# The output projection of the convolution layer, over pairs of row tiles with seven block products for eight

## The chip, the cores and the metric

The kernel runs on one core of a Trainium2 chip. The metric is the device time of one execution in microseconds (us), as the median of three runs. One execution was also taken by the hardware profiler; every time in this text comes from that execution or from the three runs.

## What is computed

Two layers over 4096 tokens with 1024 channels: each has a mixer, a gated residual, a normalisation, and a mixture of experts. The mixer of the second layer is a short convolution, and its last projection is what the change touches:

```python
def short_conv_mixer(h, w_in, conv_w, w_out):
    b_g, c_g, v = jnp.split(h @ w_in, 3, axis=-1)
    u = c_g * v
    z = lax.conv_general_dilated(u, conv_w, ...)
    return (b_g * z) @ w_out
...
    x = x + (1 + g1)[:, None, :] * out
    hn = modulate(rmsnorm(x, norm2_g[i]), sh2, sc2)
    x = x + (1 + g2)[:, None, :] * hier_moe(hn, ...)
```

The router of the mixture takes `hn`, finds for each token a group and two experts, and writes records of them.

## The kernel before

The program is a chain of phases, each behind a barrier of all engines: constants, `ssm_front`, `ssm_scan`, `project` ("glu"), `moe` ("m0"), `conv_in` ("conv"), `project` ("cout"), `moe` ("m1"). The change touches `conv_in` and the second `project`. All products are in two parts: each operand is split into a high part (ScalarE copies it with rounding) and a low part (VectorE subtracts), and `product` (L140) gives three matmuls for one block of 128 x 128 by 128 x 512.

**conv_in.** It computes `h @ w_in`, the convolution and the gate `b_g`, and writes the result transposed to the DRAM tensor `zT`. Its second part is a list of `OPS` = 84 operations, n = 0 to 83, in 12 groups g of seven (r = n mod 7), 36 matmuls each: the first four groups are of column chunk 1, the next of chunk 2, the last of chunk 3. They are themselves seven products for eight (class `Seven`): the sums of the inputs are made by GpSimd (`combine`), sums of the weights too (`small_mix`). In each group VectorE adds banks into kept sums, and after r = 1, 4, 5 and 6 it has a column tile of z ready; GpSimd stores the four tiles (`store(g, 0)` to `store(g, 3)`). SyncE loads the operand of n + 4 when product n is through, ScalarE makes the high part of n + 2 during n, VectorE the low part. PSUM has two sets of three banks, so product n waits until VectorE has read what product n - 2 left. Near the end SyncE also loads the weight of the next phase (`n_raw`, eight slices, straight from the input `conv_w_out`), ScalarE and VectorE split it (L2689, L2988), and the first source tile likewise.

**project, "cout".** It runs over 32 tiles of 128 tokens. For each, TensorE makes two banks (`cout_pM`, 2 x 512 columns) of 8 products, that is 48 matmuls. VectorE multiplies by the gate `1 + g1` (L1447), adds the residual (L1449), squares and sums (L1451), normalises (L1459, L1461), and makes the low part of the next source tile (L1434). TensorE transposes the normalised rows (`turned_hn`, L1694) and multiplies them with the router (`router_halves` L1710, `router_sum` L1719). After every four tiles VectorE runs `choose` (a chain of some 35 small operations on the logits) and then, after two matmuls of TensorE (`batch_ranks`), `place`; GpSimd stores the records. The order on each engine is that of the code; each body is written out for all tiles.

## Time and profile before

| | us |
|---|---|
| median of three runs | 6161.75 |
| lowest, highest | 6160.59, 6164.22 |
| the profiled execution | 6154.4 |
| its span | 6152.6 |
| TensorE busy | 5849.7 (95% of the span) |
| VectorE busy | 3795.6 (62%) |
| GpSimd busy | 2086.2 (34%) |

Starts are in us from the span's start. The convolution's 84 operations run from 3494 to 4187, phase "cout" from 4196 to 4658, and the last mixture follows. A row of the timeline has start, duration, engine, line, operation, tiles, and in brackets how long the engine was idle before it and what ended that. TensorE's matmuls overlap: the distance from start to start is what one costs.

### The profile page before, as it was taken

What the parts mean: (1) busy time and instruction counts of PE and PEld (TensorE: products, weight loads), DVE (VectorE), ACT (ScalarE), POOL (GpSimd) and SP (SyncE); (2) the same over time, 40 slices, a digit from 0 to 9 for tenths busy, and PEclk for the clock granted to TensorE, in tenths of its full rate; (3) what the DMA queues carried; (4) which work ended last, traced back from release to release, by engine and by line L of the source; (5) the groups of instructions that cost most, each with busy time, mean ns of one, the idle gap of its engine ahead of it and who ended that gap; (6) DMA issues with size and microseconds to landing.
All of it is one profiled execution on the core that took longest, in us unless ns stands there. A gap on an engine that the chain in (4) does not pass through costs nothing. (4 is left out here: it accounts for less than half of the span.)

```text
span 6152.6 us, 83067 instructions
## 1 busy us (share of the span) xinstructions
PE 5849.7 (95%) x28274; PEld 4775.9 (78%) x28275; DVE 3795.6 (62%) x5360; ACT 2133.1 (35%) x3188; POOL 2086.2 (34%) x1978
## 2 busy tenths in 40 slices
PE   7999989999899999999989999998997999999994
PEld 5876668888678888888868788887775888888884
DVE  6889945554455555555536688876776554556555
ACT  2334432222144334444335323321113333444434
POOL 6555538870122222222324533101112222223222
PEclk9999999999899999999999999999998999999997
DMA  4564664432267666767647756644445656777767
GB/s 153 175 193 150 189 230 148 140 135 83 84 220 214 204 174 209 217 201 212 188 132 269 268 184 202 198 156 162 152 155 191 194 163 188 212 214 244 212 199 282
DMA packets 621295, 1152.42 MB, mean 187 GB/s; under 512 B 122708, under 2 KB 219572, under 8 KB 620089
## 3 DMA queue, kind: packets, MB, share of 16 engines
q1 hardware_dynamic: 422256, 799.04, 38.0%
q0 software_dynamic: 94176, 315.82, 18.8%
q10 hardware_dynamic: 104682, 35.19, 2.2%
q8 instruction: 109, 1.79, 0.1%
q14 instruction: 72, 0.59, 0.0%
HBM read 863.32 MB, written 286.29 MB: 187 GB/s over the span
## 5 line engine op out<-in xcount | busy, mean ns | idle before, releaser
L2288 DVE SCALAR_TENSOR_TENSOR m_o<-m_pO,m_weight_of,m_gate 128x512 f32<-128x512 f32 x316 | 233.6, 746 | 714.1 <-POOLq L1933 377.4
L2255 DVE TENSOR_TENSOR m_w_lo<-m_w_raw,m_w_hi 128x1024 fp32r<-128x1024 f32 x512 | 596.1, 1214 | 0.1
L1915 POOL COPY m_gather_now<-m_gather_of 128x1 int32 (+1 forms) x161 | 182.5, 1133 | 1147.0 <-DMA x<-m_o,m_scatter_now 913.7
L2086 ACT ACTIVATE m_xT_hi<-m_pX 128x512 fp32r<-128x512 f32 x320 | 191.4, 599 | 1000.3 <-PE m_pB L146 994.3
L144 PE MATMUL m_pA<-m_w_lo,m_xT_hi 128*128 128x512 f32 x1280 | 517.4, 404 | 14.2 <-DVE m_xT_lo L2266 14.2
L2074 ACT ACTIVATE m_w_hi<-m_w_raw 128x1024 fp32r<-128x1024 f32 x512 | 505.6, 1053 | 50.3 <-DMA m_w_raw<-in_moe_w_dram 29.2
L2027 PE MATMUL m_pO<-m_w_lo,m_hT_hi 128*128 128x512 f32 x1280 | 514.1, 402 | 0.4 <-ACT m_hT_hi L2091 0.2
L146 PE MATMUL m_pA<-m_w_hi,m_xT_hi 128*128 128x512 f32 x1280 | 503.0, 393 | 0.0
L145 PE MATMUL m_pA<-m_w_hi,m_xT_lo 128*128 128x512 f32 x1280 | 500.4, 391 | 0.0
L2027 PE MATMUL m_pO<-m_w_hi,m_hT_hi 128*128 128x512 f32 x1280 | 499.9, 391 | 0.0
L144 PE MATMUL m_pB<-m_w_lo,m_xT_hi 128*128 128x512 f32 x1280 | 498.3, 389 | 0.0
L146 PE MATMUL m_pB<-m_w_hi,m_xT_hi 128*128 128x512 f32 x1280 | 498.2, 389 | 0.0
L145 PE MATMUL m_pB<-m_w_hi,m_xT_lo 128*128 128x512 f32 x1280 | 498.1, 389 | 0.0
L144 PE MATMUL glu_pM<-glu_w_lo,glu_sT_hi 128*128 128x512 f32 x1024 | 409.6, 400 | 2.8 <-DVE glu_w_lo L1542 2.8
L145 PE MATMUL glu_pM<-glu_w_hi,glu_sT_lo 128*128 128x512 f32 x1024 | 401.1, 392 | 0.0
L146 PE MATMUL glu_pM<-glu_w_hi,glu_sT_hi 128*128 128x512 f32 x1024 | 400.2, 391 | 0.0
L144 PE MATMUL conv_p<-conv_op_lo,conv_w_hi 128*128 128x512 f32 x1008 | 392.7, 390 | 5.6 <-DVE conv_op_lo L2922 5.6
L145 PE MATMUL conv_p<-conv_op_hi,conv_w_lo 128*128 128x512 f32 x1008 | 392.3, 389 | 0.0
L146 PE MATMUL conv_p<-conv_op_hi,conv_w_hi 128*128 128x512 f32 x1008 | 392.3, 389 | 0.0
L2261 DVE TENSOR_TENSOR m_w_lo<-m_w_raw,m_w_hi 128x1024 fp32r<-128x1024 f32 x256 | 306.2, 1218 | 74.8 <-issue 63.4
L1401 POOL DMA_INDIRECT slots<-route_record,route_place x120 | 124.6, 1038 | 662.7 <-DVEq L1527 628.4
L2031 PE MATMUL m_pO<-m_w_hi,m_hT_lo 128*128 128x512 f32 x1280 | 342.6, 390 | 0.0
(531 smaller groups left out, 13591.2 us busy)
## 6 DMA issues: line engine op xcount, KB each, us to landing
m_w_raw<-in_moe_w_dram SPq DMA_DIRECT2D x384, 1024.0 KB, 7.4
conv_op_raw<-xr SPq DMA_DIRECT2D x84, 1024.0 KB, 5.4
glu_ada<-in_ada_w_dram POOLq DMA_DIRECT2D x96, 256.0 KB, 3.2
a_x<-in_x_dram SPq DMA_DIRECT2D x32, 512.0 KB, 3.4
a_ada<-in_ada_w_dram POOLq DMA_DIRECT2D x64, 256.0 KB, 3.4
s_u<-u SPq DMA_DIRECT2D x64, 256.0 KB, 2.7
s_r<-k SPq DMA_DIRECT2D x64, 256.0 KB
glu_x<-in_x_dram SPq DMA_DIRECT2D x32, 512.0 KB, 5.0
```

The costliest lines, as they stand in the source:

```text
L144: pe.matmul(out, lh, rl, start=start, stop=False)
L145: pe.matmul(out, ll, rh, start=False, stop=False)
L146: return pe.matmul(out, lh, rh, start=False, stop=stop)
L1401: pool.indirect_dma_start(slots_dram, bass.IndirectOffsetOnAxis(ap=routes.place[b % 2][:, j:j + 1], axis=0), routes.record[b % 2][:, j, :] ...
L1915: pool.tensor_copy(gx[:], gidx[:, bass.ds(t, 1)]).then_inc(gi_ready, 1)
L2027: pe.matmul(pO[:, n, :], hT_hi[:, k, :], w[:, n, k, :], start=k == 0 and w is w2_low, stop=False)
L2031: last = pe.matmul(pO[:, n, :], hT_lo[:, k, :], w2_high[:, n, k, :], start=False, stop=k == KF - 1)
L2074: act.activation(W13[s][2][:, m, k:k + 2, :], W13[s][0][:, m, k:k + 2, :], ACT.Copy).then_inc(w13_hi, 1)
L2086: act.activation(xT_hi[:, 4 * q:4 * q + 4, :], pX[:, 4 * q:4 * q + 4, :], ACT.Copy).then_inc(xt_hi, 1)
L2255: tt(W13[s][1][:, m, k:k + 2, :], W13[s][0][:, m, k:k + 2, :], W13[s][2][:, m, k:k + 2, :].bitcast(F32), ALU.subtract).then_inc(w13_lo, 1)
L2261: tt(w2_low[:, n, k:k + 2, :], w2_raw[:, n, k:k + 2, :], w2_high[:, n, k:k + 2, :].bitcast(F32), ALU.subtract).then_inc(w2_lo, 1)
L2288: dve.scalar_tensor_tensor(out=ob[:, n, :], in0=pO[:, n, :], scalar=wslot[:, bass.ds(tile_, 1)], in1=gate2[:, n, :], op0=ALU.mult, op1=ALU ...
```

## The change

For each pair of tiles (2p, 2p + 1) the projection is a 2 x 2 by 2 x 2 product of blocks: rows are the odd and the even tile, the inner dimension its two halves of 512, columns the two halves of the output. The changed kernel makes it with seven block products (84 matmuls) for eight (96).

- **Weights.** The block operands (four blocks of the weight and four sums, each [512, 512]) are made by GpSimd during the convolution, in 16 steps `turn(i)`, four in each of the groups 7 to 10, with the factor `1 + g1` multiplied in, and written to the new DRAM tensor `wt`. A step waits until both stores of the step before it have landed, loads two pieces of the weight and a piece of the gate, computes six operations, and stores twice.
- **The end of conv_in.** SyncE waits at n = 78 for the last of these stores, and then loads the weights 0 and 1 of the seven, then the operand of n = 83, and later weights 2 and 3 and two source tiles. ScalarE splits weight 0 at n = 79, 1 at 81, 2 at 82, VectorE behind it; weights 3 to 6 are split in the next phase, 4 to 6 also loaded there.
- **The projection** is a new function `project_out`. Four banks of 512 columns go round; product m waits until bank m - 4 is read. VectorE makes four sums of source tiles, seven low parts, and the sums over banks straight into the residual rows; it no longer multiplies by the gate. The sum of squares goes to ScalarE. The routing is as before, in other places: both tiles of pair p - 1 are turned and routed during pair p, `choose` in slot 3 and `place` in slot 6 of the odd pairs from p = 3 on. After the last pair both of its tiles are still to be normalised and routed.

Core of the diff (of `project_out`, which is new, the parts of VectorE and TensorE):

```diff
@@ conv_in, GpSimd
+            def turn(i):
+                kk, q = seven.turns[i]
+                (a, b_), tt = pieces, pool.tensor_tensor
+                for h in range(2):
+                    if i:
+                        pool.wait_ge(turn_st[h], 16 * i)
...
+                for h in range(2):
+                    pool.dma_start(a[:, 2 * h:2 * h + 2, :], next_view[kk][q][h]).then_inc(turn_ld, 16)
+                pool.dma_start(gate_piece[:], gate_view[q].broadcast_to([P, 2, P])).then_inc(turn_ld, 16)
+                pool.wait_ge(turn_ld, 48 * i + 48)
+                d = Chain(pool, turn_step, 6 * i)
+                d(pool.tensor_scalar(gate_piece[:], gate_piece[:], 1.0, None, ALU.add))
+                wide = a[:].rearrange("p (h n) f -> p h n f", h=2)
+                d(tt(wide, wide, gate_piece[:].unsqueeze(1).broadcast_to([P, 2, 2, P]), ALU.mult))
+                to = lambda o: wt_dram[o:o + 4, kk, :, q * P:(q + 1) * P].rearrange("o p f -> p o f")
+                pool.dma_start(to(0), a[:]).then_inc(turn_st[0], 16)
+                d(tt(b_[:, 3, :], a[:, 3, :], a[:, 1, :], ALU.subtract))
+                d(tt(b_[:, 1, :], a[:, 1, :], a[:, 0, :], ALU.subtract))
+                d(tt(b_[:, 0, :], b_[:, 3, :], a[:, 0, :], ALU.add))
+                d(tt(b_[:, 2, :], a[:, 2, :], b_[:, 0, :], ALU.subtract))
+                pool.dma_start(to(4), b_[:]).then_inc(turn_st[1], 16)
...
+                for i in range(4 * (g - 7), 4 * (g - 6)) if 7 <= g < 11 else ():
+                    turn(i)
+                    if i % 4 == 1:
+                        store(g, 2)
@@ conv_in, SyncE
                 if n == OPS - 6:
-                    for k in range(6):
-                        sp.dma_start(n_raw[:, k, :], next_view[k]).then_inc(n_w_ld[k], 16)
+                    for q in range(2):
+                        sp.wait_ge(turn_st[q], 16 * len(seven.turns))
+                    next_weights(0)
+                    next_weights(1)
@@ conv_in, ScalarE   (NEXT_W = {OPS - 5: 0, OPS - 3: 1, OPS - 2: 2})
-                ks = {OPS - 3: range(0, 6), OPS - 2: range(6, KD)}.get(n, ())
...
+                if n in NEXT_W:
                     act.wait_ge(prod, 3 * n)
+                    act.wait_ge(n_w_ld[NEXT_W[n]], 16)
+                    act.activation(ahead.w_hi[NEXT_W[n]][:], ahead.w_raw[NEXT_W[n]][:], ACT.Copy).then_inc(n_w_hi, 1)
@@ project_out, VectorE
+            def slot(p, s):
+                q, r = next_left(p, s)
...
+                if s == 0:
+                    if p:
+                        left_sums(p, 4)
+                        odd_done(p - 1)
+                        low(p, 6)
+                        normed(p - 1, 0)
...
+                elif s == 3:
+                    from_bank(p, 2, u2[:], kept[:])
+                    if more:
+                        low(q, r)
+                    if batch_at(p) is not None:
+                        choose(batch_at(p))
...
+                else:
+                    from_bank(p, 5, xe[:, B], xe[:, B])
...
+                    if p:
+                        out_logits(2 * (p - 1))
+                    if batch_at(p) is not None:
+                        place(batch_at(p))
@@ project_out, TensorE
+            def turned_hn(n):
+                pe.wait_ge(hn_ready, n + 1)
+                if n:
+                    pe.wait_ge(lg_out, n)
+                if n % 2 and batch_at((n + 1) // 2) is not None:
+                    pe.wait_ge(r_out, batch_at((n + 1) // 2) + 1)
...
+                    if p and r == 6:
+                        turned_hn(2 * (p - 1) + 1)
```

Three places where instructions move. On GpSimd in `conv_in`, from the stores of group 6 on (`conv_z` is a column tile, `ws` takes weight sums of the convolution). Before:

```order
L2855 DMA ws<-conv_small_15309 256x1x256
L2834 DMA zT<-conv_z 128x512 x20
L2478 UNCONDITIONAL_BRANCH
```

and now, from the same store on through the first step and a half (`conv_piece` holds the four pieces, `wt` is the new tensor):

```order
L3409 DMA ws<-conv_small_15352 256x1x256
L3364 DMA zT<-conv_z 128x512 x4
L3383 DMA conv_piece_15391<-in_conv_w_out_dram 128x2x128 x2
L3384 DMA conv_gate_piece<-mod 128x2x128
L3387 TENSOR_SCALAR conv_gate_piece<-conv_gate_piece 128x256
L3389 TENSOR_TENSOR conv_piece_15391<-conv_piece_15391,conv_gate_piece 128x512
L3391 DMA wt<-conv_piece_15391 128x4x128
L3392 TENSOR_TENSOR conv_piece_15392<-conv_piece_15391 128x128
L3393 TENSOR_TENSOR conv_piece_15392<-conv_piece_15391 128x128
L3394 TENSOR_TENSOR conv_piece_15392<-conv_piece_15392,conv_piece_15391 128x128
L3395 TENSOR_TENSOR conv_piece_15392<-conv_piece_15391,conv_piece_15392 128x128
L3396 DMA wt<-conv_piece_15392 128x4x128
```

GpSimd had nothing but twenty stores left; now 16 such steps stand between them.

On SyncE at the end of `conv_in`. Before, and then now (`conv_op_raw` is the operand of one of the 84 operations, n = 81 to 83 here):

```order
L2551 DMA conv_op_raw1_15337<-xr 128x4x512
L2551 DMA conv_op_raw2_15338<-xr 128x4x512
L2591 DMA ahead_raw_49<-in_conv_w_out_dram 128x1024 x6
L2551 DMA conv_op_raw3_15339<-xr 128x4x512
L2594 DMA ahead_raw_49<-in_conv_w_out_dram 128x1024 x2
```

```order
L3072 DMA conv_op_raw1_15380<-xr 128x4x512
L3072 DMA conv_op_raw2_15381<-xr 128x4x512
L3075 DMA ahead_w_raw0_49<-wt 128x4x512
L3075 DMA ahead_w_raw1_52<-wt 128x4x512
L3072 DMA conv_op_raw3_15382<-xr 128x4x512
L3121 DMA ahead_src0_91<-zT 128x8x128
```

The weight loads ahead of the last operand now read what GpSimd writes.

On ScalarE there, before and then now (`conv_op_hi` is a high part; slots 2 and 3 are n = 82 and 83):

```order
L2633 ACTIVATE conv_op_hi1_15345<-conv_op_raw1_15337 128x1024 x2
L2633 ACTIVATE conv_op_hi2_15346<-conv_op_raw2_15338 128x1024 x2
L2633 ACTIVATE conv_op_hi3_15347<-conv_op_raw3_15339 128x1024 x2
L2689 ACTIVATE ahead_hi_51<-ahead_raw_49 128x1024 x6
```

```order
L3164 ACTIVATE conv_op_hi1_15388<-conv_op_raw1_15380 128x1024 x2
L3218 ACTIVATE ahead_w_hi0_51<-ahead_w_raw0_49 128x2048
L3164 ACTIVATE conv_op_hi2_15389<-conv_op_raw2_15381 128x1024 x2
L3222 ACTIVATE ahead_left_hi0_72<-ahead_src0_91 128x512
L3222 ACTIVATE ahead_left_hi1_75<-ahead_src0_91 128x512
L3164 ACTIVATE conv_op_hi3_15390<-conv_op_raw3_15382 128x1024 x2
```

The first weight's high part has come ahead of the operands of n = 82 and 83; on VectorE its low part stands ahead of their low parts in the same way.

## Rows read from the trace of the kernel before

**Rows 1.** Busy time by engine, phase "cout" without its first tile; clock last but two.

```profile
4214.00:4640.00 426.00, 416.91 (x2320) 337.02 (x2320) 302.97 (x600) 74.36 (x152) 60.77 (x56) 1.00 0.45 151
```

**Rows 2.** Timeline of VectorE in phase "cout".

```profile
4348.14 1.22 DVE L1447 TENSOR_TENSOR cout_acc<-cout_pM,cout_gate 128x1024 f32<-128x1024 f32 x1 [1.89 <-PE cout_pM L146]
...
4383.22 0.17 DVE L1489 TENSOR_REDUCE cout_m<-cout_logits 128x4 f32<-128x16 f32 x1
...
4390.71 1.22 DVE L1447 TENSOR_TENSOR cout_acc<-cout_pM,cout_gate 128x1024 f32<-128x1024 f32 x1
...
4402.83 1.22 DVE L1447 TENSOR_TENSOR cout_acc<-cout_pM,cout_gate 128x1024 f32<-128x1024 f32 x1 [1.87 <-PE cout_pM L146]
...
4407.50 1.29 DVE L1459 SCALAR_TENSOR_TENSOR cout_hn<-cout_x,cout_stat,cout_gain 128x1024 f32<-128x1024 f32 x1
...
4416.12 1.22 DVE L1447 TENSOR_TENSOR cout_acc<-cout_pM,cout_gate 128x1024 f32<-128x1024 f32 x1 [4.84 <-PE cout_pM L146]
```

**Rows 3.** Timeline of TensorE in phase "cout", one tile and the end of another.

```profile
4399.68 0.39 PE L146 MATMUL cout_pM<-ahead_hi,next_src_hi 128*128 128x512 f32 x1
...
4402.40 0.39 PE L146 MATMUL cout_pM<-ahead_hi,next_src_hi 128*128 128x512 f32 x1
4402.63 1.03 PE L1694 MATMUL cout_pH<-ident,cout_hn 128*128 128x128 f32 x8
...
4415.93 1.03 PE L1694 MATMUL cout_pH<-ident,cout_hn 128*128 128x128 f32 x8
```

**Rows 4.** Timeline of VectorE at the end of `conv_in` and the start of "cout".

```profile
4186.57 0.68 DVE L2971 TENSOR_TENSOR conv_c<-conv_p,conv_kept 128x512 f32<-128x512 f32 x1
4187.17 0.68 DVE L2971 TENSOR_TENSOR conv_v<-conv_p,conv_kept 128x512 f32<-128x512 f32 x1
4187.88 0.69 DVE L2979 TENSOR_TENSOR conv_u<-conv_c,conv_v 128x512 f32<-128x512 f32 x1
...
4191.63 0.69 DVE L2984 TENSOR_TENSOR conv_z<-conv_z,conv_b 128x512 f32<-128x512 f32 x1
4195.76 3.59 DVE L1530 TENSOR_TENSOR ahead_lo<-ahead_raw,ahead_hi 128x1024 fp32r<-128x1024 f32 x3 [3.44 <-PEq L105]
```

**Rows 5.** Timeline of GpSimd: `store(7, 1)` and `store(10, 1)`.

```profile
3944.57 0.54 POOL L2834 DMA_DIRECT2D zT<-conv_z  x1 [23.94 <-DVE conv_z L2984]
...
4115.92 0.54 POOL L2834 DMA_DIRECT2D zT<-conv_z  x1 [23.94 <-DVE conv_z L2984]
```

**Rows 6.** Groups of GpSimd in `conv_in`: count, busy us, mean ns, idle before.

```profile
L2809 POOL TENSOR_TENSOR conv_mix<-conv_mix 128x512 f32<-128x512 f32 x16 | 24.6, 1536 | 1.3
...
L2852 POOL TENSOR_TENSOR conv_small<-conv_small 128x128 f32<-128x128 f32 x24 | 20.2, 840 | 1.9
...
L2855 POOL DMA_DIRECT2D ws<-conv_small x24 | 16.7, 695 | 7.9 <-POOL conv_small L2854 7.9
L2851 POOL TENSOR_TENSOR conv_small<-conv_small 128x128 f32<-128x128 f32 x24 | 15.5, 646 | 6.7 <-DMA conv_small<-in_conv_w_in_dram 6.5
```

**Rows 7.** DMA issues: count, KB each, median us from issue to landing.

```profile
conv_op_raw<-xr SPq DMA_DIRECT2D x84, 1024.0 KB, 5.4
...
conv_small<-in_conv_w_in_dram POOLq DMA_DIRECT2D x48, 128.0 KB, 3.2
ws<-conv_small POOLq DMA_DIRECT2D x24, 256.0 KB, 2.8
```

**Rows 8.** TensorE after a pause: timeline in `conv_in` and the last mixture, and a window.

```profile
3533.49 0.50 PE L144 MATMUL conv_p<-conv_op_lo,conv_w_hi 128*128 128x512 f32 x1 [3.37 <-DVE conv_op_lo L2922]
...
6072.10 1.11 PE L2015 MATMUL m_pH<-ident,m_h 128*128 128x128 f32 x4 [4.22 <-DVE m_h L2274]
...
6072.00:6076.00 4.00, 3.76 (x10) 2.82 (x11) 2.16 (x6) 3.10 (x7) 0.53 (x1) 0.50 1.01 406
```

**Rows 9.** The end of "cout": TensorE after its last products, and VectorE's last operation.

```profile
4634.79 1.03 PE L1694 MATMUL cout_pH<-ident,cout_hn 128*128 128x128 f32 x8
...
4658.19 0.17 DVE L1526 CAST route_place<-route_place_f 128x8 int32<-128x8 f32 x1
```

More of the change, by code:

```diff
@@ L1275, in project @@
     records_of = lambda b: 16 * sum(len(routes.columns(c)) for c in range(b % 2, b + 1, 2))
[L1276 removed]
+    pad_st = sem("pad_stored")
     with ExitStack() as ctx:
@@ L1535, in _ @@
             chosen(dve.tensor_scalar(routes.base[:], io32[:], float(T), None, ALU.mult))
-            if glu:
-                low(0, 0)
-            else:
-                dve.sem_inc(tlo[0], 1)
-            for q in range(KD if glu else 0):
+            low(0, 0)
+            for q in range(KD):
                 dve.wait_ge(w_hi_ready, q + 1)
@@ L1654, in products @@
                 pe.wait_ge(tlo[s], i + 2)
-                if not glu:
-                    pe.wait_ge(out_read, n + 1)
-                elif not (isinstance(n, int) and n == 0):
+                if n != 0:
                     pe.wait_ge(gated, 2 * n)
-                first, second = ((1, 0), (2, 0)) if glu else ((0, KD // 2), (1, 0))
                 def rest():
@@ L2433, in __init__ @@
         assert not sums and not mixes
+        self.turns = [(kk, q) for kk in range(KH) for q in range(4)]
         self.small = [(c, kk, j) for c in range(2, CHUNKS) for kk in range(KH) for j in range(3)]
@@ L2582, in _ @@
                 again = seven.sb(n) == SUPER - 1 and seven.chunk(n) + 1 < NC_
-                if more or again or n in (OPS - 6, OPS - 4):
+                if more or again or n in range(OPS - 6, OPS - 2):
                     sp.wait_ge(prod, 3 * n + 3)
@@ L2867, in _ @@
                         store(g, 1)
+                for i in range(4 * (g - 7), 4 * (g - 6)) if 7 <= g < 11 else ():
+                    turn(i)
+                    if i % 4 == 1:
+                        store(g, 2)
+                if g not in range(7, 11) and g + 1 < OPS // SEVEN:
+                    store(g, 2)
                 if g + 1 < OPS // SEVEN:
-                    store(g, 2)
                     store(g, 3)
@@ L2998, in _ @@
                     all_mixed(dve, 1)
-                ahead = n + 2 < OPS
-                if ahead:
+                follows = n + 2 < OPS
+                if follows:
                     op_low(n + 2, 0)
@@ L3004, in _ @@
                         summed(n, i, r - 2, kept[r - 1][JS[i]])
-                        if ahead and i == 0:
+                        if follows and i == 0:
                             op_low(n + 2, 1)
@@ L3018, in _ @@
                     column_out(n, q, base + first + 3 * by)
-                elif ahead:
+                elif follows:
                     op_low(n + 2, 1)
```

719 lines of the change are left out of this document (580 added, 139 removed).

## The prediction, made before the changed kernel ran

> **What bounds the kernel now.** I read the busy times by stretch first. In phase "cout" TensorE is busy 416.91 of 426 us at full clock and VectorE 302.97 [rows 1]: TensorE bounds, VectorE has 29% left. TensorE's timeline gives the prices. Between 4399.68 and 4402.40 lie 12 matmul starts, so a matmul costs 0.227 us; a tile takes 13.30 us [rows 3], of which 48 matmuls are 10.9 and the routing (8 transposes, 16 + 2 small products, changes between them) 2.4. VectorE's timeline shows the rest: an ordinary tile keeps it 13.29 - 4.84 = 8.45 us; `choose` runs from 4383.22 to 4390.71, 7.5 us, and the tile with `place` takes 12.12 - 1.87 = 10.25, so `place` is 1.8 [rows 2]. From 4348.14 to 4402.83, four tiles with one `choose`, pass 54.7 us and not 4 x 13.3 = 53.2: the chain behind `choose` already costs TensorE 1.5 us. In the convolution's last groups TensorE bounds too, an operation being 36 x 0.227 = 8.16 us, a group of seven 57.1, which GpSimd's stores confirm: (4115.92 - 3944.57) / 3 = 57.1 [rows 5]. GpSimd is idle between them. So there are two questions: does TensorE remain the bound of the projection, and do the new steps on the idle GpSimd end in time.
>
> **The steps on GpSimd.** `turn(i)` hides nothing of its own latency: loads, operations, stores and the next step's first wait follow one another. Its parts: three DMA issues, the last 1.1 us after the first (0.54 each, as [rows 5]), and 3.2 until it lands [rows 7], 4.3; one operation on 256 columns and one on 512, between 0.65 and 0.84 for 128 columns and 1.54 for 512 [rows 6], so 0.8 + 1.4, 0.3 before the store's issue; the issue 0.7 [rows 6]; four operations of 128 columns at a mean of 0.65 to 0.84, with gaps 3.2; 0.3, and 2.8 until the second store lands [rows 7]. Sum 13.8; the stores here are in pieces half as long, I add 0.4: **14.2 us**. With every part at its shortest I get 11.6, with queues 15.5.
>
> Four steps and the four stores of z among them, 56.8 + 2.2 = 59.0, against a group of 57.1: the steps of group 7 begin at 3945.1 (behind `store(7, 1)`), those of 8, 9 and 10 each 1.9 late or later. The last store lands at R = 3945.1 + 3 x 59.0 + 57.4 = 4179.5. SyncE, however, waits for it from n = 78, whose product is through at about 4145.6 (that of n = 74 ended some 3 us before `store(10, 1)` at 4115.92, and four operations of 8.16 follow). Behind that wait stand weight 0, weight 1, and the operand of n = 83; behind weight 0 stands ScalarE at n = 79, ahead of the operand of n = 82; behind ScalarE VectorE. So operation 82, due three operations later at 4170, cannot start before R and what follows. From R on: weight 0 lands after 5.4 [rows 7], with two loads behind it 6.4; its high part takes ScalarE 2.0 (no row has 2048 columns; VectorE's 1024 take 1.2 [rows 4]); then VectorE is the chain. It has three low parts of weights at 2.3, 6.9; four halves of operands at 1.14, 4.6; three column tiles at 4186.57 to 4192.32, 5.75 each [rows 4], 17.3; six more bank sums and two source low parts at 0.6, 4.8; 33.6 in all. Then 3.4 to the next phase [rows 4]. It starts at R + 45.4 = 4224.9 instead of 4195.7: **+29.2 us**. The bounds follow from the step: at 11.6 nothing slips from group to group, R = 4116.5 + 47.0 = 4163.5, and the phase starts 13.2 late; at 15.5, R = 4200 and it starts 50 late. Were the steps done by 4145, the start would be 2.3 early, since VectorE has one weight to split at n = 82 for three slices before. I take 14.2, nearest to the median landings.
>
> Here the Trainium skill speaks for a shorter step ("DMA: Bandwidth & Descriptors", section "Anatomy of one DMA"): it gives a DMA about 2.0 us fixed and bytes at 436 GB/s. By that, 128 KB would be 2.3 and 256 KB 2.6, the step 12.7 and the phase 17.6 late, not 29.2; the trace's landings of 3.2 and 2.8 are longer, and the sum goes by them.
>
> **The projection.** Removed from TensorE: 12 matmuls in a pair, 2.72 us, over 16 pairs 43.6. That is hidden unless VectorE keeps up. Its queue for a pair, by start-to-start distances of 512 columns: 0.60 where the next one doesn't wait for it (4186.57 to 4187.17), 0.71 to 0.73 where it does [rows 4], some 0.1 more where a semaphore is raised between. Seven low parts 4.2; four sums of sources 2.6, and behind the third 0.7 in which ScalarE makes the high part that the next low part needs; seven reads of banks 4.9; kept and second sums 2.7; two normalisations of 1.29 + 1.22 and a small one, 5.3 [rows 2]; logits 0.2. In all **20.7 us a pair**, against TensorE's 84 x 0.227 + 4.8 = 23.9. But two pairs hold a `choose` and a `place`: VectorE 50.7, TensorE 47.8. And the waits couple the two closely: TensorE may not turn the second tile of pair p - 1 (behind product 6 of pair p) before VectorE's `out_logits` and, in odd pairs, the start of `place` in its slot 6. So an odd pair is VectorE's: 20.7 + 7.5 + 0.4 = 28.6 from such a turn to the next, in which TensorE stands about 4.3 us in one piece; an even pair is TensorE's, 24.0. Two pairs: **52.6** against 54.7 before.
>
> The phase: from its start to the turn in pair 2 about 79 us (the first seven products wait for weights 4, 5 and 6, whose low parts are ready near 15, 19 and 24 us, by 1 MB loads at 5.4 and more and 2.3 on VectorE for each; pair 1 is then VectorE's). Then seven odd and six even pairs, 200.2 + 144.0, to 423. The tail: before, 4634.79 to 4658.4, 23.6 [rows 9]. Now both tiles of the last pair are still to be normalised and routed: one normalisation more (2.7) and the short `choose` of two tiles (6.4) stand on the chain that was hidden, less 1: 31.7. The phase is 455 us, before 4658.4 - 4195.7 = 462.7: **-7.7**. The bound below is a TensorE at 47.8 for two pairs throughout; that is a rival. Above: 10 us more at the start if loads take the longer times.
>
> **TensorE's clock.** A pause of 3.37 us left it at full clock; behind one of 4.22 the granted clock was 0.50 in 6072 to 6076 [rows 8], that is 1.2 of 2.4 GHz, and nine matmuls at twice the distance, with slower transposes, cost 2.2 us. The new pauses of about 4.3 us, eight with that of pair 1, lie at that edge, and the even pair after each is TensorE's, so such a loss counts. I take half of them: **+9**, between 0 and 18.
>
> **The sum**, on the profiled execution's own time of 6154.4: + 29.2 - 7.7 + 9 = 6184.9; its median over runs lies 7.35 higher, so **6192 us**.
>
> **Rivals.**
> - *Steps in time.* If four steps end within some 30 us behind `store(10, 1)`, SyncE waits for nothing, the phase starts 2.3 early, and the projection with the clock is about even: 6161. For it: GpSimd is empty, and the shortest small operations and landings. Against: the sum of even the shortest parts is 11.6, four of them 47.
> - *The projection is TensorE's after all*, the one on the other side: VectorE's two pairs fall below 47.8 us. Then 8 x 4.9 = 39 less and no pauses: 6192 - 39 - 9 = 6144, faster in spite of the late steps. It decides at 3 us in 50.7, 6% of VectorE's work; for it speaks that VectorE's chained operations may overlap more than I let them; against, that rows of the same width repeat within 0.01 us.
> - *All pauses lower the clock, and the steps take 15 us or more*: 50 - 7.7 + 18, and the start's 10: 6222 at the worst, 6207 as its middle. The Trainium skill ("TensorE: Matmul & The Clock Gate", section "Why this matters for your kernels") warns of this: bursts of matmuls with pauses between fall to half clock each time. The row at 4.22 agrees, the one at 3.37 doesn't.
> - *The waits of VectorE on the stores of z.* `store(g, 3)` now stands behind four steps. With 59 us a group it lands some us before VectorE needs the tile again; with 62 it doesn't, and the delay adds to the third rival.
>
> **How the numbers follow.** Late steps and VectorE-bound pairs 0.62; the third rival 0.14; steps in time 0.15; TensorE-bound 0.07; the remaining 0.02 for less than 6149. The likeliest gives 6192. Its own range, from R at 11.6 us a step without losses of clock (6154.4 + 7.35 + 13.2 - 7.7 - 5 = 6162) to 15.5 with half of them (6215), is also where 8 in 10 lie: **6160 to 6215**. A measurement of this kernel tells about 0.2%, 12 us, from no change. Faster than 6149.4: 0.07 + 0.02, of which some ends above, 0.07. Within: most of "steps in time" and the low end of the likeliest, 0.17. Slower than 6174: 0.76.
>
> **What would show it.** Right: the four `turn` steps of a group last 50 to 60 us; SyncE's load of weight 0 starts after 4163 and TensorE is idle before operation 82; phase "cout" starts after 4208; in the odd pairs from 3 on TensorE has one pause of 4 to 5 us before the transposes, and VectorE none; two pairs take 52 to 53 us. Wrong: a step of 10 us or less (the first part falls); VectorE idle in the odd pairs, or 48 us for two (the second falls); a clock of 1.00 behind all pauses takes 9 us off, 0.50 behind each puts 9 on.

## The result

The changed kernel takes 6222.7 us in the median of four runs (6216.3 to 6232.8), the kernel before 6161.3 beside it: 1.0100 times as long (95% interval 1.0083 to 1.0118), **61.4 us slower**. Slower was forecast, but as 6192 (6160 to 6215): half the size. The profiled execution of the changed kernel took 6223.35 us, with a span of 6221.4 against 6152.6. The 68.8 us between the two profiles fall so:

| | forecast | measured |
|---|---|---|
| already there at `store(7, 1)`, ahead of the first step | 0 | 3.5 |
| later start of phase "cout", less that | +29.2 | +62.1 |
| the phase, from the barrier ahead of it to the first product of the last mixture, with the clock | -7.7 + 9 | +1.2 |
| the last mixture | 0 | +2.0 |

The 3.5 lie ahead of the first step. That they belong to the change isn't shown: among the experiments below, kernels whose code up to this point is the same have it anywhere from 3948.8 to 3955.1, and the profiled execution of the kernel before, at 6154.4, is 6.2 us below the lowest of its three runs.

First the steps. Timeline of GpSimd (start, duration, engine, line, what, and in brackets the idle time before and what ended it): the first step with the start of the second, then the last step.

```profile
3948.10 0.54 POOL L3364 DMA_DIRECT2D zT<-conv_z  x1 [23.94 <-DVE conv_z L3543]
3948.65 1.44 POOL L3383 DMA_DIRECT2D conv_piece<-in_conv_w_out_dram  x2
...
3955.38 0.94 POOL L3387 TENSOR_SCALAR conv_gate_piece<-conv_gate_piece 128x256 f32<-128x256 f32 x1 [4.59 <-DMA conv_gate_piece<-mod]
...
3962.95 0.78 POOL L3396 DMA_DIRECT2D wt<-conv_piece  x1 [0.29 <-POOL conv_piece L3395]
3969.83 1.42 POOL L3383 DMA_DIRECT2D conv_piece<-in_conv_w_out_dram  x2 [6.10 <-DMA wt<-conv_piece]
...
4203.61 1.42 POOL L3383 DMA_DIRECT2D conv_piece<-in_conv_w_out_dram  x2 [2.74 <-DMA wt<-conv_piece]
...
4208.46 0.85 POOL L3387 TENSOR_SCALAR conv_gate_piece<-conv_gate_piece 128x256 f32<-128x256 f32 x1 [2.73 <-DMA conv_gate_piece<-mod]
...
4214.14 0.80 POOL L3396 DMA_DIRECT2D wt<-conv_piece  x1 [0.29 <-POOL conv_piece L3395]
```

The first step takes 21.2 us, the last, until its stores have landed, 13.6. The four steps of groups 7 to 10 begin at 3948.65, 4020.11, 4092.11 and 4158.41: 71.5, 72.0 and 66.3 us for a group that I had at 59.0 and that the convolution passes in 57.1 [rows 5]. What happens behind the last store, SyncE, ScalarE, VectorE and TensorE:

```profile
4217.24 0.91 SPq L3075 DMA_DIRECT2D ahead_w_raw<-wt  x2
...
4222.91 1.91 ACT L3218 ACTIVATE ahead_w_hi<-ahead_w_raw 128x2048 fp32r<-128x2048 f32 x1 [64.75 <-DMA ahead_w_raw<-wt]
...
4224.86 2.29 DVE L3547 TENSOR_TENSOR ahead_w_lo<-ahead_w_raw,ahead_w_hi 128x2048 fp32r<-128x2048 f32 x1 [47.35 <-ACT ahead_w_hi L3218]
...
4230.07 0.80 PE L143 MATMUL conv_p<-conv_op_lo,conv_w_hi 128*128 128x512 f32 x1 [38.65 <-DVE conv_op_lo L3481]
...
4261.36 0.76 PE L143 MATMUL cout_p<-ahead_w_lo,ahead_left_hi 128*128 128x512 f32 x1 [12.19 <-PEq L104]
```

The chain is the one forecast: the last store lands and SyncE passes its wait at R = 4217.2, weight 0 lands, ScalarE, VectorE, and only then operation 82, for which TensorE stood 38.65 us. The phase starts at R + 44.1; the forecast was R + 45.4. R itself was forecast as 4179.5. Ahead of that VectorE had waited twice for a store of z behind the steps, 15.0 and 15.6 us, and TensorE behind it, 5.5 and 7.0; since the last step ends later still, this costs nothing more:

```profile
4158.32 0.49 DVE L3456 TENSOR_SCALAR conv_z<-conv_u,conv_taps 128x512 f32<-128x512 f32 x1 [15.59 <-DMA zT<-conv_z]
```

```profile
4161.16 0.79 PE L143 MATMUL conv_p<-conv_op_lo,conv_w_hi 128*128 128x512 f32 x1 [6.98 <-DVE conv_b L3530]
```

Now the projection. TensorE's turns of the second tile of pairs 2 and 14, and the busy times of the same middle of the phase as [rows 1] (PE, PEld, DVE, ACT, POOL; clock last but two):

```profile
4345.01 1.04 PE L2187 MATMUL cout_pH<-ident,cout_hn 128*128 128x128 f32 x8
...
4668.93 1.03 PE L2187 MATMUL cout_pH<-ident,cout_hn 128*128 128x128 f32 x8
```

```profile
4345.00:4450.00 105.00, 99.02 (x536) 79.54 (x535) 91.76 (x186) 37.69 (x68) 19.66 (x16) 0.93 0.45 152
4450.00:4560.00 110.00, 103.75 (x571) 83.48 (x570) 96.42 (x195) 41.41 (x76) 19.41 (x16) 0.97 0.48 162
```

Six times two pairs in 323.9 us, **54.0 us for two pairs** (four at 54.3 to 54.5, two at 53.2) against 52.6 forecast and 54.7 before [rows 2]. VectorE is busy 87% of the time, 71% before [rows 1]. An odd pair, TensorE:

```profile
4365.70 0.39 PE L145 MATMUL cout_p<-ahead_w_hi,ahead_left_hi 128*128 128x512 f32 x1
4369.08 0.64 PE L2210 MATMUL cout_pH<-cout_selector,cout_logitsT 100*128 100x36 f32 x2 [2.99 <-ACT cout_logitsT L2110]
...
4370.38 0.77 PE L143 MATMUL cout_p<-ahead_w_lo,ahead_left_hi 128*128 128x512 f32 x1
4370.95 0.63 PE L144 MATMUL cout_p<-ahead_w_hi,ahead_left_lo 128*128 128x512 f32 x1
...
4375.22 0.45 PE L145 MATMUL cout_p<-ahead_w_hi,ahead_left_hi 128*128 128x512 f32 x1
```

There is one pause, but not where I had it (before the transposes behind product 6): it is at `router_sum` behind product 5, and 2.99 us long. Behind it matmuls lie 0.43 apart and not 0.23, eleven of them: half of the full clock, 1.2 and not 2.4 GHz (the granted clock is 0.55 as a mean from 4369 to 4376). ScalarE's queue tells why, with VectorE's beside it:

```profile
4368.23 0.63 ACT L2080 ACTIVATE ahead_left_hi<-ahead_left_raw 128x512 fp32r<-128x512 f32 x1 [7.80 <-DVE ahead_left_raw L1933]
4368.77 0.26 ACT L2110 ACTIVATE cout_logitsT<-cout_pH 100x128 f32<-100x128 f32 x1
```

```profile
4358.01 0.16 DVE L1879 TENSOR_REDUCE cout_m<-cout_logits 128x4 f32<-128x16 f32 x1
...
4365.31 0.17 DVE L1904 TENSOR_SCALAR route_record<-route_token 128x8 f32<-128x8 f32 x1
...
4367.51 0.69 DVE L1933 TENSOR_TENSOR ahead_left_raw<-ahead_src,ahead_src 128x512 f32<-128x512 f32 x1
```

`choose` holds VectorE from 4358.01 to 4365.5, so the sum for block 3 of the next pair (L1933) is late; ScalarE waits 7.80 us for it with the high part (L2080), and the copy that TensorE wants (L2110) stands behind.

### The profile page after: what moved, and what is told of

It is laid out like the page before. It is cut to its first block and busy times, and to the rows that moved or that the text cites. A ratio compares the mean times of both kernels' runs of the same rounds, so it can differ in the third digit from the quotient of the medians.

```text
span 6221.4 us, 83117 instructions
## 1 busy us (share of the span) xinstructions
PE 5840.9 (94%) x28082; PEld 4760.3 (77%) x28083; DVE 3883.0 (62%) x5503; ACT 2219.2 (36%) x3316; POOL 2230.7 (36%) x2153
## 5 line engine op out<-in xcount | busy, mean ns | idle before, releaser
L2574 ACT ACTIVATE m_w_hi<-m_w_raw 128x1024 fp32r<-128x1024 f32 x512 | 505.7, 1053 | 49.7 <-DMA m_w_raw<-in_moe_w_dram 27.9
L2766 DVE TENSOR_TENSOR m_xT_lo<-m_pX,m_xT_hi 128x512 fp32r<-128x512 f32 x320 | 220.2, 689 | 184.0 <-ACT m_xT_hi L2586 184.0
```

Of the source, the lines that this page charges most:

```text
L2574: act.activation(W13[s][2][:, m, k:k + 2, :], W13[s][0][:, m, k:k + 2, :], ACT.Copy).then_inc(w13_hi, 1)
L2766: tt(xT_lo[:, 4 * q:4 * q + 4, :], pX[:, 4 * q:4 * q + 4, :], xT_hi[:, 4 * q:4 * q + 4, :].bitcast(F32), ALU.subtract).then_inc(xt_lo, 1)
```

## The experiments

Theory: the loss is the length of the steps and nothing else, and the projection is bound by VectorE. All kernels below come from the changed one; e2 to e7 and e9 to e11 also have the spread steps of e1, and each diff shows only what is new against the kernel named. Beside them the kernel before had 6160.9 (e0 to e3), 6162.2 (e4 to e7) and 6159.9 us (e8 to e11). "The phase" is from the barrier ahead of it to the first product of the last mixture: 464.1 us before, 465.3 changed. (In the changed kernels the phase's first product follows the barrier at once; in the kernel before it came 4.4 us later, at 4200.08.)

### Steps: e0, e1, e8

**e0_loads_ahead** has the loads of step i + 1 ahead of the work of step i:

```diff
+                if i + 1 < len(seven.turns):
+                    turn_load(i + 1)
-                pool.wait_ge(turn_ld, 48 * i + 48)
+                pool.wait_ge(turn_ld[i % 2], 48 * (i // 2) + 48)
```

> The changed kernel with one edit on GpSimd: the pieces have two pairs of buffers, and a step issues the loads of the step after it before it computes; the 16 steps stay in groups 7 to 10. My theory is that the length of a step sets the delay of phase cout. A step is now its issues (2.1), six operations (some 5.5 with gaps) and two stores' issues (1.6) without the waits for its load and for the stores of the step before: about 10 us for 16.8. Then no group slips, the last store lands near 4165, SyncE passes its wait 52 us earlier than 4217, phase cout starts at 4209 for 4261, and the run takes 6170 us (6160 to 6182) for 6223. Rival: the delay lies in the transfers (1 MB operands and pieces share the DMA engines) and in what stands behind SyncE's wait; then a shorter step gains less than half of it, and the run stays above 6195.

Measured 6190.9 us (6188.2 to 6199.2): between the two. My step was wrong: the loads of step i + 1 use the buffers of step i - 1, whose stores have only just been issued. The wait for the load is gone, the one for the stores is longer, as GpSimd's timeline shows (last store of a step, start of the next), and a step beside the convolution still takes 15.9 us. SyncE's first load of a weight and TensorE's first product of the phase below it:

```profile
3966.85 0.78 POOL L3411 DMA_DIRECT2D wt<-conv_piece  x1 [0.30 <-POOL conv_piece L3410]
3974.77 1.42 POOL L3390 DMA_DIRECT2D conv_piece<-in_conv_w_out_dram  x2 [7.14 <-DMA wt<-conv_piece]
...
4194.80 0.91 SPq L3077 DMA_DIRECT2D ahead_w_raw<-wt  x2
...
4239.00 0.77 PE L143 MATMUL cout_p<-ahead_w_lo,ahead_left_hi 128*128 128x512 f32 x1 [12.72 <-PEq L104]
```

What the theory says of everything behind the steps holds: R is 22.4 us earlier, the phase starts 22.4 earlier, at R + 44.2.

**e1_turns_early** spreads the steps:

```diff
-                for i in range(4 * (g - 7), 4 * (g - 6)) if 7 <= g < 11 else ():
-                    turn(i)
...
+                        if g in (3, 7, 8, 9):
+                            turn(turned_)
+                            turned_ += 1
                         store(g, 0)
+                        if g in (1, 2, 3, 5, 6, 7, 8, 9):
+                            turn(turned_)
+                            turned_ += 1
                         store(g, 1)
+                if g in (3, 7, 8, 9):
+                    turn(turned_)
+                    turned_ += 1
```

> The changed kernel with the 16 steps unchanged but spread: two buffers of their own, and one step in each of groups 1, 2, 5 and 6, three in each of groups 3, 7, 8 and 9, so that the last ends near 4110. Theory: SyncE waits for nothing at n = 78, phase cout starts at 4197 to 4200, all of the late steps' cost is gone and the projection is what remains: +62 of the +61 us lie in the steps, the projection with its clock losses is within 3 us of the old one, and the run takes 6158 us (6150 to 6166), as the kernel before. Rival: the steps also cost VectorE or the DMA queues something in the convolution wherever they stand: then 6170 or more. In the trace the projection keeps two pairs of 54.4 us with one pause of 2.99 us each.

Measured 6159.0 us (6156.3 to 6164.8), 0.9995 times the kernel before (0.9986 to 1.0005). The phase starts at 4201.3 and takes 465.0, the changed kernel's 465.3. (Expected was a start at 4197 to 4200; counted from `store(7, 1)`, 248.3 us against 251.2 in the kernel before, it is 2.9 early.) So the whole 61 us of the change are the steps that end late, and with them in time the projection gains nothing. The rival, a cost of the steps wherever they stand, is not seen.

**e8_three_a_group** is a dose between: `{3: 4, 7: 3, 8: 3, 9: 3, 10: 3}` steps by group, all behind `store(g, 1)`.

> The changed kernel with the 16 steps unchanged, in their own buffers, four in group 3 and three in each of the groups 7 to 10, all behind store(g, 1) as before. It is a dose between e1_turns_early (none late) and the changed kernel (four a group). Theory: three steps of 17 us and the stores take 53 us, less than a group of 57.1, so that no group slips; the last three begin near 4120 and end near 4171, SyncE passes its wait there, and phase cout starts 44.2 us later, as it did behind 4217.2 and 4194.8: 4213 to 4218, 15 us after that of e1_turns_early; run 6171 to 6178 us. Rival: the first late step costs as much as all four (the pause and its clock are the price, not its length): 6200 or more; or nothing, 6160.

Measured 6177.2 us (6173.0 to 6181.3), in the range. R is 4173.4, the phase starts at 4217.4, R + 44.0. Over all three doses each us of R is one us of the kernel: from the changed kernel to e8 R is 43.9 us earlier and the median 45.4 lower. The one between is not on this line: R falls by 22.4 to e0 and by 21.4 from there, the median by 31.8 and 13.7. R is read in one execution, and e0's, at 6199.2, is the slowest of its four; between the profiled executions the differences are 24.2 and 24.0.

### The order of the projection: e2, e3, e4, e7, e9

**e2_scalar_order** (from e1):

```diff
-                if s == 5 and p:
+                if p and s == (4 if batch_at(p) is not None else 5):
                     out_lT(2 * (p - 1))
```

> As e1_turns_early, and in the odd pairs with choose ScalarE copies the routing sums (cout_logitsT) ahead of the high part of the next pair's block 3, which waits for VectorE behind choose. It is this order at which TensorE pauses 2.99 us now. Theory: VectorE is the bound of the odd pair whatever ScalarE does; the pause goes to the transposes behind product 6, which wait for place, about 3.4 us long, with the same loss of clock behind it; two pairs stay at 53.5 to 54.5 us and the run within 4 us of e1_turns_early. Rival: the pause was ScalarE's order alone; then two pairs take 48 to 50 us, and the run 30 to 40 us less than e1_turns_early.

Measured 6165.6 us (6158.4 to 6168.1), 6.6 more than e1 where at most 4 were expected; two pairs take 54.0 to 54.9. The pause did go to the transposes, 4.07 us long. **e3_own_banks** (from e2) takes away this wait:

```diff
+        pL, pR = (core.ps(ctx, f"{tag}_{n}", [P, 4, P]) for n in ("pL", "pR"))
...
             def turned_hn(n):
                 pe.wait_ge(hn_ready, n + 1)
-                if n:
-                    pe.wait_ge(lg_out, n)
-                if n % 2 and batch_at((n + 1) // 2) is not None:
-                    pe.wait_ge(r_out, batch_at((n + 1) // 2) + 1)
```

> As e2_scalar_order, and the routing's sums, logits and ranks have two PSUM banks of their own, so that TensorE's transposes wait neither for VectorE's reading of the logits nor for place. Theory: what is left is the amount of VectorE's work, 50.8 us in two pairs (54.4 less the 3.6 that it is idle in the even pair) against TensorE's 47.8; two pairs take 51 to 52 us, pauses get short, most of the clock's loss of 2.6 us in a pair is gone, and the run takes 15 to 20 us less than e2_scalar_order. Rival: another wait takes the place of it (a bank, a low part) with the same pause: 54 us, no gain. A result of 48 us in two pairs would say that VectorE's work was never the bound.

Measured 6164.6 us (6160.1 to 6167.7), two pairs 54.7: no gain, the rival. **e4_scalar_order2** (from e3) takes away the wait that came in its place:

```diff
+                late = batch_at(p - 1) is not None
+                if s == 0 and p >= 2 and late:
+                    out_h(2 * (p - 2) + 1)
                 if s == 0 and p:
                     high(p, 6)
-                    if p >= 2:
+                    if p >= 2 and not late:
                         out_h(2 * (p - 2) + 1)
```

> As e3_own_banks, and behind an odd pair with choose ScalarE copies the turned rows (cout_hT) ahead of the high part of block 6, which waits for VectorE. In e3_own_banks TensorE paused 4.93 us for this copy. Theory: with this no queue stands between TensorE and its own work, only the amount of VectorE's work, 50.8 us in two pairs, is left, and two pairs take 51 to 52 us instead of 54.75; run 6142 to 6150 us. Rival: the pause moves again at the same size (54.5 or more, 6164 us): then each reordering only chooses where TensorE waits for the same VectorE, and the odd pair's surplus and the clock behind the pause set the time, not the sum over two pairs.

Measured **6142.5 us** (6139.5 to 6148.4), 0.9972 (0.9960 to 0.9983). The pause of an odd pair in e2, e3 and e4 (the last two pairs later), TensorE:

```profile
4311.91 1.30 PE L2187 MATMUL cout_pH<-ident,cout_hn 128*128 128x128 f32 x5 [4.07 <-DVEq L1912]
```

```profile
4312.93 1.87 PE L2203 MATMUL cout_pL<-cout_hT,cout_router 128*36 128x128 f32 x16 [4.93 <-ACT cout_hT L2108]
```

```profile
4360.54 1.07 PE L2206 MATMUL cout_pL<-cout_hT,cout_router 128*36 128x128 f32 x16 [1.21 <-ACT cout_hT L2108]
```

The pause went from `router_sum` to the transposes (waiting for `place`), and from there to the routing's product (waiting for ScalarE behind VectorE's sum), each time a little longer; with the third wait gone it is 1.2 to 1.6 and 1.3 us in two pieces, the clock stays full, and two pairs take 51.2 us. That is close to VectorE's own work as estimated, 50.8. The first two edits gave nothing without the third; whether the third would give it without them is not tested.

**e9_split_alone** cuts `choose` in two (below) on top of e4, with all work still on VectorE.

> As e4_scalar_order2 with choose cut in two as in e6_choose_split, but the sums of source tiles stay on VectorE. Theory (the sum of VectorE's work over two pairs is the bound): 50.8 to 51.3 us for two pairs as in e4_scalar_order2, run 6139 to 6146 us, since nothing leaves VectorE. Rival (the odd pair's surplus was the bound, and the cut is what helped in e6_choose_split): two pairs at 49.5 us or less and the run at 6130 us or less.

Measured 6141.7 us (6138.2 to 6147.5), two pairs 51.2. As the theory has it: moving work between pairs gives nothing while its sum is the bound.

**e7_filler** (from e1) asks what the clock alone costs:

```diff
+                        if batch_at(p) is not None and p + 1 < PAIRS:
+                            for k in range(11):
+                                pe.matmul(fill[:], w_hi[0][:, k % KH, 0:P], w_hi[0][:, k % KH, :], start=True, stop=True)
                         router_sum(2 * (p - 1))
```

> As e1_turns_early (not the ones behind it), and TensorE makes 11 more matmuls of 512 columns, 2.5 us, into a bank that nobody reads, just where it pauses 2.99 us in the odd pairs. It does the same work otherwise. Theory on the clock: the pause of 2.99 us costs twice, itself and then 2.4 to 2.6 us because the next 12 matmuls take 0.427 instead of 0.227 us; with the filler the pause is 0.5 us, the clock stays at 1.00, and two pairs take 51.6 to 52 us instead of 54.4; the run takes 13 to 17 us less than e1_turns_early, 6142 to 6146 us. Rival (VectorE is the bound of both pairs together, so a faster TensorE only waits elsewhere): less than 5 us. Second rival: the clock falls all the same, since VectorE and not TensorE's idleness brings it down: no gain at all.

Measured 6156.4 us (6154.6 to 6160.4), the phase 460.2 for 465.0. TensorE in one odd pair:

```profile
4308.95 0.41 PE L2210 MATMUL cout_pH<-cout_selector,cout_logitsT 100*128 100x36 f32 x2 [0.49 <-ACT cout_logitsT L2110]
...
4313.45 1.06 PE L2187 MATMUL cout_pH<-ident,cout_hn 128*128 128x128 f32 x8 [0.80 <-DVEq L1912]
...
4317.94 1.07 PE L2202 MATMUL cout_pH<-cout_hT,cout_router 128*36 128x128 f32 x16 [0.64 <-ACT cout_hT L2106]
```

The clock was full throughout (1.00 from 4283 to 4608), but of the 2.4 us of slow matmuls only 1.2 come back: with fast matmuls TensorE meets two new waits on VectorE's side, 0.80 and 0.64. Two pairs take 53.2, not 51.6 to 52. The run is 2.6 us under e1 and not 13 to 17: the first rival, less than 5. The clock cost 4.8 us of the phase in these two profiled executions, and 2.6 between the medians (3.9 if each is set against the kernel before beside it).

### Work off VectorE: e5, e6, e10, e11

**e5_sums_gpsimd** (from e4) moves the four sums (L1925 to L1938) to GpSimd.

```diff
                     if more:
                         low(q, r)
-                        left_sums(q, 1)
-                        left_sums(q, 2)
...
+            for p in range(1, PAIRS):
+                left_sum(p, 4)
+                for which in (1, 2) if p + 1 < PAIRS else ():
+                    left_sum(p + 1, which)
```

> As e4_scalar_order2, and GpSimd makes the four sums of source tiles of each pair from the second on, with its 512-column operations of some 1.5 us (6 of 24 us a pair). VectorE loses 5.3 us of 50.8 in two pairs and the waits of 0.7 for the high parts behind its own sums. Theory (VectorE's work is the bound): TensorE's 47.8 us is the bound of two pairs, with a short pause in the odd pair: 48 to 50 us, the run 6120 to 6135 us, clearly under the kernel before. Rival: VectorE and GpSimd slow each other (in the convolution an operation of VectorE took 1.69 for 1.22 us beside GpSimd's), or a sum comes late: two pairs stay above 51.5 us and the run above 6145.

Measured 6145.9 us (6142.0 to 6147.8): no gain, two pairs 52.4. The rival, and in both of its halves. A sum comes late: GpSimd makes the third one behind its eight stores of records, and in every two pairs VectorE waits once for ScalarE's high part of it:

```profile
4433.86 0.69 DVE L1976 TENSOR_TENSOR ahead_left_lo<-ahead_left_raw,ahead_left_hi 128x512 fp32r<-128x512 f32 x1 [2.93 <-ACT ahead_left_hi L2111]
```

And the two engines slow each other. Groups of VectorE from 4392 to 4500 (count, busy us, mean ns, idle before), e4 and then e5:

```profile
L1943 DVE TENSOR_TENSOR ahead_left_lo<-ahead_left_raw,ahead_left_hi 128x512 fp32r<-128x512 f32 x8 | 5.5, 693 | 3.4 <-ACT ahead_left_hi L2082 2.8
L1952 DVE TENSOR_TENSOR cout_x_even<-cout_p,cout_x_even 128x512 f32<-128x512 f32 x8 | 5.5, 682 | 0.0
L1959 DVE SCALAR_TENSOR_TENSOR cout_hn<-cout_x_odd,cout_stat,cout_gain 128x1024 f32<-128x1024 f32 x4 | 5.1, 1286 | 0.1
L1959 DVE SCALAR_TENSOR_TENSOR cout_hn<-cout_x_even,cout_stat,cout_gain 128x1024 f32<-128x1024 f32 x4 | 5.1, 1285 | 0.1
```

```profile
L1976 DVE TENSOR_TENSOR ahead_left_lo<-ahead_left_raw,ahead_left_hi 128x512 fp32r<-128x512 f32 x8 | 8.5, 1058 | 6.5 <-ACT ahead_left_hi L2111 5.9
L1992 DVE SCALAR_TENSOR_TENSOR cout_hn<-cout_x_even,cout_stat,cout_gain 128x1024 f32<-128x1024 f32 x4 | 8.4, 2111 | 0.1
...
L1985 DVE TENSOR_TENSOR cout_x_even<-cout_p,cout_x_even 128x512 f32<-128x512 f32 x8 | 5.5, 682 | 0.0
```

Operations of VectorE that read two tiles in SBUF grow where GpSimd works beside them: 0.69 to 1.06, 1.29 to 2.11 (the same normalisation of the odd row, in another place, keeps its 1.29). Those that read a bank (L1952, L1985) do not. Over the four groups that grow it is 10.4 us in 108, where the sums taken away were 12.4. Counted over whole pairs nothing is left of the gain: VectorE is busy 46.7 us in two pairs in e4 and 46.7 in e5. The Trainium skill states such a lock ("SBUF — State Buffer", section "SBUF: two separate sides": an operation of VectorE with two SBUF inputs and one of GpSimd hold a pair of ports in turn, for a whole instruction); the rows agree.

**e11_idle_adds** (from e4) measures that price alone, with four additions a pair on a buffer of no use.

```diff
+                pool.wait_ge(prod, 7 * p)
+                for _ in range(3):
+                    e(pool.tensor_tensor(idle[:], idle[:], idle[:], ALU.add))
...
+                pool.wait_ge(prod, 7 * p + 4)
+                e(pool.tensor_tensor(idle[:], idle[:], idle[:], ALU.add))
```

> As e4_scalar_order2, and GpSimd makes four additions of 512 columns in each pair on a buffer that nobody uses. It measures alone what such an operation costs VectorE, on which nothing waits here. Theory: while GpSimd's operation runs, a VectorE operation with both inputs in SBUF is held until it ends; eight of them in two pairs lengthen VectorE's work by about 0.6 us each, 5 us, as the rows of e5_sums_gpsimd had it (low parts 1.06 for 0.69, normalisation 2.11 for 1.29): two pairs 55 to 57 us for 51.2, run 6165 to 6180 us. Rival: the longer operations in e5_sums_gpsimd were those that waited for a sum: then 51.2 and 6142 us here.

Measured 6162.2 us (6159.0 to 6168.3), 19.7 more than e4, and 54.15 us for two pairs, 2.95 more: under the expected 55 to 57, but not the rival's 51.2. The lock is there though nothing waits for these operations; each of the eight costs 0.37 us, less than the 0.6 that I took from e5. VectorE's busy time in two pairs goes from 46.7 to 49.7 and the two pairs longer by the same, which shows that VectorE sets their time. (The stores of records stand between the additions here; they are the same ones as in e4.)

```profile
L1955 DVE TENSOR_TENSOR ahead_left_lo<-ahead_sum,ahead_left_hi 128x512 fp32r<-128x512 f32 x9 | 8.6, 957 | 0.3
L1955 DVE TENSOR_TENSOR ahead_left_lo<-ahead_left_raw,ahead_left_hi 128x512 fp32r<-128x512 f32 x8 | 6.1, 768 | 3.4 <-ACT ahead_left_hi L2094 2.8
```

**e6_choose_split** (from e5):

```diff
                     if batch_at(p) is not None:
-                        choose(batch_at(p))
+                        choose(batch_at(p), (0,) if p < PAIRS - 1 else (0, 1))
+                    if place_at(p) is not None and p < PAIRS - 1:
+                        choose(place_at(p), (1,))
```

> As e5_sums_gpsimd, and choose is cut in two: the part that reads the logits (3.1 us) stays in slot 3 of the odd pair, the rest (4.3 us) and place come in the even pair behind it. VectorE then has some 21.2 us in the odd and 24.3 us in the even pair against TensorE's 23.9 in each. Theory: no pause of TensorE above 1 us in the middle of the phase, granted clock 1.00 there, two pairs 47.8 to 48.5 us, run 6112 to 6125 us. Rival: the odd pair's surplus was absorbed by the four banks already in e5_sums_gpsimd: no difference between the two.

Measured **6130.3 us** (6124.4 to 6134.8), 0.9949 (0.9932 to 0.9966), above the 6112 to 6125 expected. Two pairs take 48.2 and 48.5 at first and 49.4 from pair 7 on: no pause of TensorE is over 0.5 us between 4250 and 4590, and VectorE is busy 93% of the time. Against e9, which differs only in who makes the sums, that is 1.8 us less in two pairs and 11.4 in the run, although VectorE is as busy as there (46.7 for 46.8 in two pairs); what is shorter is its idle time, 2.8 for 4.5, of which 1.4 were the two waits for ScalarE's high part behind its own sums. What is left between 49.4 and TensorE's 47.8 I did not take apart. **e10_records_last** puts the stores of records behind the third sum:

> As e6_choose_split, and GpSimd issues the eight stores of records (10 us) behind the third sum of the next pair instead of ahead of it. In e5_sums_gpsimd VectorE waited 2.93 us for that sum. Theory: two pairs 48.5 to 49 us for 49.45, run 6124 to 6129 us. Rival: in e6_choose_split the sum was in time, since place stands elsewhere there: no difference (within 3 us).

Measured 6128.1 us (6125.8 to 6130.6), 0.9947 (0.9929 to 0.9965), two pairs 49.7 and not 48.5 to 49: its rival, no difference. Either is 0.5% faster than the kernel before: the fastest version of this study.

## Why the prediction was wrong

**The steps (+29.2, measured +62.1): the term that failed.** The failing step is the sum for one `turn`, 14.2 us. That sum is right for a GpSimd that is alone. The last three steps begin at 4175.27, when SyncE has issued its last load of an operand (before 4167.1) and VectorE is about to stand still (from 4177.5; TensorE from 4191.4), and R is 4217.24: 14.0 each. Some of that agreement is luck: in the last step the load with its issues took 4.85 us and not 4.3, the four operations of 128 columns 2.1 and not 3.2. For the 0.4 that I added for shorter pieces no run has a measurement of its own; the second store took 3.1 from issue to landing, where 3.2 were in the sum. The thirteen ahead of them, beside the convolution, take (4175.27 - 3948.65) / 13 = **17.4 us**. Groups of GpSimd, steps 0 to 12 and then 13 to 15 (count, busy us, mean ns, idle before):

```profile
L3389 POOL TENSOR_TENSOR conv_piece<-conv_piece,conv_gate_piece 128x512 f32<-128x512 f32 x13 | 19.5, 1497 | 1.1
...
L3387 POOL TENSOR_SCALAR conv_gate_piece<-conv_gate_piece 128x256 f32<-128x256 f32 x13 | 13.5, 1042 | 47.4 <-DMA conv_gate_piece<-mod 47.4
...
L3395 POOL TENSOR_TENSOR conv_piece<-conv_piece,conv_piece 128x128 f32<-128x128 f32 x13 | 9.4, 720 | 1.0
```

```profile
L3389 POOL TENSOR_TENSOR conv_piece<-conv_piece,conv_gate_piece 128x512 f32<-128x512 f32 x3 | 3.8, 1272 | 0.2
L3387 POOL TENSOR_SCALAR conv_gate_piece<-conv_gate_piece 128x256 f32<-128x256 f32 x3 | 2.5, 847 | 8.2 <-DMA conv_gate_piece<-mod 8.2
...
L3395 POOL TENSOR_TENSOR conv_piece<-conv_piece,conv_piece 128x128 f32<-128x128 f32 x3 | 1.4, 457 | 0.2
```

Beside the convolution the wait for the load is 47.4 / 13 = 3.6 us against 2.7, the six operations take 1.1 us more in all, and the wait for the stores, with the stores of z issued in it, is 1.4 longer: three parts of about one us. I had taken durations of [rows 6] and medians of [rows 7] as if a step met each of them once, and none of the step's own neighbours. That the operations grow beside VectorE's two-input operations fits e5 and e11, and the first step shows it row by row, VectorE and GpSimd:

```profile
3960.33 2.01 DVE L3476 TENSOR_TENSOR conv_w_lo<-conv_w_raw,conv_w_hi 128x1536 fp32r<-128x1536 f32 x1
```

```profile
3960.80 1.85 POOL L3395 TENSOR_TENSOR conv_piece<-conv_piece,conv_piece 128x128 f32<-128x128 f32 x1
```

The subtraction takes 0.46 alone; here it ends 0.3 us behind VectorE's operation. That the landings grow by the operands' loads of 1 MB is only argued; no run takes these loads away. From 14.2 to 17.4 seems little. But a group of four then passes its 57.1 us by 9 to 15 and not by 1.9, and these slips stand one for one in R: 4217.2 for 4179.5. The start of the phase follows: 37.7 late in R, less the 3.5 from before and the 1.3 by which the chain behind R is shorter, is the 32.9 between +29.2 and +62.1. My upper bound of the step, 15.5, came from the same rows and was too low; with 17.4, which has the stores of z in it, the forecast's own working gives R = 3945.1 + 4 x 4 x 17.4 = 4223.5, with the 3.5 from before and 10 off for the three quick steps 4217. The estimate of the step by the Trainium skill's figures ("DMA: Bandwidth & Descriptors", section "Anatomy of one DMA") was 12.7, further off than the rows.

**What stands behind the steps: right.** R + 45.4, measured 44.1, 44.2 and 44.0 at three values of R.

**The projection and the clock (-7.7 and +9, together +1.3; measured +1.2).** Right in sum by luck, and only partly in its parts. That VectorE would be the bound of two pairs and eat the gain of the twelve matmuls is what e4, e9 and above all e11 show; I had its work at 50.7 us, and e4 runs at 51.2. The place of the pause was wrong: I had followed the waits of TensorE on VectorE, not those of TensorE on ScalarE on VectorE. With these queues two pairs take 53.2 us even at full clock (e7), 2 more than without them (e4). The clock fell behind all six pauses of the middle, though they were 2.99 us and not 4.3; I had taken 3.37 us as harmless from one row [rows 8]. Its price was 5 us of the phase (e7) and not 9, because half of it lies in a wait for VectorE; two pairs without it take 53.2 and not 52.6, which gives nearly all of that back. The start of the phase, to the turn in pair 2, took 83.7 us for 79, and what follows the turn in pair 14 took 57.7, where the forecast's terms, counted to the same point, make 61.7: these two errors cancel.

**The rivals.** *Steps in time* (6161) is e1 to 2 us; its condition was not met by far. *TensorE-bound after all* was not seen in any version for long: two pairs at 48.2 us stand once, at the start of e6 and of e10, and 49.4 and 49.7 behind them. *All pauses lower the clock and steps of 15 us or more* (6207 to 6222) is what happened, at its upper end, by longer steps and not by the clock; its 6222 is too low by its own terms, since 50 - 7.7 + 18 alone give it and the start's 10 would make 6232. *VectorE waits for stores of z*: it did, for 15 us twice, and TensorE with it for 12.5 together; but it added nothing to the third rival as I had said, because SyncE's wait for R ends later and covers it.

## What to carry to other kernels

A chain of small steps on an idle engine is priced by its length beside the others' work, and first by whether a group of them fits in its period: once a group of them does not fit, each us that a step is longer comes back times the number of all steps, sixteen here. Before a step is made shorter it can be started earlier, in any free time ahead of it; here that was worth the 64 us between the changed kernel and e1. And when a reorder removes a pause, one asks which queue the same producer reaches next: the first two removals gave nothing, and the third, on top of them, gave 22 us.

## What the runs showed of the hardware

- GpSimd and VectorE are not free of each other: 1.3 us additions of GpSimd cost VectorE 0.37 us each (e11), and moving 12.4 us of sums to GpSimd lengthened VectorE's other operations by 10.4 in the four groups shown (e5), its busy time in two pairs staying at 46.7. Operations with an input in PSUM kept their 0.68.
- How far TensorE's clock falls behind a pause isn't told by the pause alone. Behind 2.99 us the changed kernel had eleven slow matmuls in four pairs, and four and eight in the two others; only the pairs with eleven took longer, 54.4 for 53.2 us. In e8, whose projection is the same code at another time, the first such pause, one of 2.98 us, left full clock, and so did the third:

```profile
4323.88 0.41 PE L2210 MATMUL cout_pH<-cout_selector,cout_logitsT 100*128 100x36 f32 x2 [2.98 <-ACT cout_logitsT L2110]
```

  Only its last had eleven slow matmuls, and its phase took 460.2 us, as with the filler, for 465.0 in e1: 3.7 of these 4.8 us are three times two pairs at 53.2 for 54.4, with the same pauses at another time. In e10 a shorter pause, one of 2.01 us, had four slow matmuls behind it (granted clock 0.76 from 4376 to 4383):

```profile
4378.70 1.88 PE L2242 MATMUL cout_pL<-cout_hT,cout_router 128*36 128x128 f32 x16 [2.01 <-ACT cout_hT L2144]
```
